# Two decoder layers on one core: both output projections as three float32r products by column halves, with the expert weights loaded at half way and at the last product

## The chip, the cores and the metric

The kernel runs on one core of one Trainium2 chip. The metric is the device time of one execution in microseconds (us), the median of several runs. The core has five engines that run at the same time: TensorE (PE, matrix products into PSUM), VectorE (DVE), ScalarE (ACT), GpSimd (POOL) and SyncE (SP), which here issues nearly all transfers. Sixteen DMA engines move the data between HBM and SBUF.

## What is computed

A causal decoder trunk of two layers over 512 tokens of width 1024, all in float32. Each layer does

```
x = layer_norm(ALPHA * x + mixer(x) @ w_out)
x = layer_norm(ALPHA * x + hierarchical_moe(x))
x = x + sigmoid(x @ w_gate) * (p @ w_proj)
```

In layer 0 the mixer is a retention with four heads beside a causal pooling mixer in four groups; their eight blocks of 128 features form the 1024 features that `ab_w_out` (1024 x 1024) maps. In layer 1 it is a sparse attention with 16 heads over the top 128 keys; `c_w_out` (1024 x 1024) maps its output. The mixture of experts sends each token to two of 32 experts; an expert is a 1024 x 1024 matrix `moe_w_gu` (4.19 MB) and a 512 x 1024 matrix `moe_w_down` (2.10 MB). The kernel loads all 32 experts of a layer.

## The kernel before

The kernel is written engine by engine, in stages; each stage is a block with a barrier at its end, and waits inside it are counts on semaphores. The stages are, for layer 0: the input projection, retention and pooling, the output projection, and routing with the experts; for layer 1: latents and indexer, attention, the output projection, and routing with the experts. P = 128, T = 4 tiles of tokens, KD = 8 blocks of features, NB = 512.

**Split products.** A float32 product on TensorE is two instructions per 512 columns here. The input projection (`split`, line 315 and line 346) and the second output projection use another form: each operand is a high part, which is its copy in the type float32r, and a low part, which is operand minus high part; the product is high x high + high x low + low x high, three float32r instructions. ScalarE makes the high parts (L321, L1964), VectorE (L350) or GpSimd (L1979) the low ones.

**Input projection.** 20 jobs of 128x512 sums on TensorE (L412), five column chunks of four jobs; ScalarE (L334) and VectorE (L376) empty the banks. Jobs 0 to 19 are counted by `pj`.

**Retention and pooling** (L472 to L563). TensorE computes scores (L500), outputs (L507), the pooling maps (L488) and the turned heads (L492). Maps and turned heads pass one after another through PSUM bank 7 in the order of the list `LAST`. TensorE may write job j there only when job j-1 is emptied, and ScalarE empties it with the gain as scale into `MT`, which is `XT` (L557). ScalarE also computes the square root of the variances (L562). VectorE normalises each head (L545) and multiplies with the swish gate (L548). SP loads the two column halves of `ab_w_out`, and then expert 0.

**Output projection** (`out_projection`, L623). For each tile t and column half c, TensorE sums the products of 8 blocks of features (L647) into bank 2t+c. VectorE adds them to ALPHA times x (L670), takes statistics, and normalises a tile when both halves are there (`Norm.dve_tile`, L199: L205, L208, L209). TensorE then turns the tile (L169), ScalarE copies it to `XT` (L176), and TensorE computes the router's logits (L640). The logits of tile t-2 stand behind the first half of tile t, the turn of tile t-1 behind its second. SP loads the router's weights, `load_third_gu` (expert 2 into w3 and w4), and some tables, stores each normalised tile to `x_rows` in HBM (L702), and then issues `then_load`: expert 1, and in layer 1 experts 0 and 1. SP ends the block only when all four stores have landed; it doesn't wait for expert weights.

**Experts.** Routing is a chain on VectorE (L782 to L857). GpSimd then gathers the tokens of an expert from `x_rows` (L883), TensorE turns them (L895) and computes with them (L910, L924). `load_gu` (L436) loads a gate-and-up matrix in two halves of 2.10 MB, `load_dn` (L440) a down matrix of 2.10 MB. There are two buffers for experts: `pair[0]` is wide[1] with slim[0], `pair[1]` is wide[0] with slim[1]; expert 2 uses w3, w4 and `XT`. From expert 3 on, SP issues each piece when TensorE has read the piece that lies in its place. L1163 is the first product behind the last expert.

Of the kernel before, what the change touches and what calls it, by code (L numbers as in the profile page):

```python
# [13 lines left out]
F32 = mybir.dt.float32  # L14
# [8 lines left out]
P = 128  # L23
# [27 lines left out]
def build(nc, A, out):  # L51
    ctx = ExitStack()
    ctx.enter_context(nc.allow_non_contiguous_dma(reason="small vectors to one feature per partition"))
    with ctx:
# [6 lines left out]
        def again(name, of, first, n):  # L61

            return nc.alloc_sbuf_tensor_at(name, [P, n], F32R, offset=home[of] + 4 * first)
# [187 lines left out]
        s_wh, s_wl = sem("w_high"), sem("w_low")  # L251

# [10 lines left out]
        with ExitStack() as first:  # L263
            def early(name, shape, dt=F32):
                return first.enter_context(nc.sbuf_tensor(name, shape, dt))
# [4 lines left out]
            XH, XL = early("x_high", [P, KD, SEQ], F32R), early("x_low", [P, KD, SEQ], F32R)  # L270
            with nc.Block() as block:
                @block.sync
                def _(sp):
# [15 lines left out]
                    sp.dma_start(DEC, A["c_decay"].rearrange("h p n -> p h n")).then_inc(s_dec, 16)  # L289

# [8 lines left out]
                def _(act):  # L299
# [26 lines left out]
                    for j in range(PROJ):  # L326
                        if j % 4 == 0 and 1 <= j // 4 < 4:
                            split(j // 4 + 1)
                        if pj_owner[j] != "act":
# [5 lines left out]
                           .then_inc(pj.sem_of(j), 1)  # L335

                @block.vector
                def _(dve):
# [30 lines left out]
                    for j in range(PROJ):  # L369
# [7 lines left out]
                        if 4 <= j < 12:  # L377
# [4 lines left out]
                            pool_group((j - 4) // 2)  # L382

# [37 lines left out]
        w_out0 = [three(slim[1][:, :], NB), three(wide[0][:, 0:4096], NB)]  # L421
# [37 lines left out]
        MT = XT  # L459
# [10 lines left out]
        mt = Jobs("mixed", ["act"] * len(LAST))  # L470

        with nc.Block() as block:  # L472
            @block.sync
            def _(sp):
                sp.dma_start(PW, A["pool_w"][0].rearrange("g c d -> c g d")).then_inc(s_pool, 16)
                sp.dma_start(w_out0[0], rows(A["ab_w_out"][0, :, 0:NB], NB)).then_inc(s_wout[0], 16)
                sp.dma_start(w_out0[1], rows(A["ab_w_out"][0, :, NB:D], NB)).then_inc(s_wout[1], 16)
                load_gu(sp, 0, 0, 0)
                load_dn(sp, 0, 0, 0)
# [38 lines left out]
            def _(dve):  # L518
                own = Own(dve, "own_ret")
                dve.wait_ge(s_dec, 16)  # L520
                for h in range(RH + 1):
# [8 lines left out]
                    if h >= 1:  # L530
# [17 lines left out]
                        dve.tensor_tensor(RN[:, :, hs], RN[:, :, hs], SG[:, :, hs], ALU.mult).then_inc(s_rn, 1)  # L548

            @block.scalar  # L550
            def _(act):
                act.wait_ge(s_const, 80)
                act.wait_ge(s_gain, 32)
                for j, (kind, i) in enumerate(LAST):
                    mt.wait_full(act, j)
                    k = i if kind == "turn" else 4 + i
                    act.activation(MT[:, k, :], PS[:, 7, :], ACT.Copy, scale=gains[:, k:k + 1])\  # L557
                       .then_inc(mt.sem_of(j), 1)
# [64 lines left out]
        def out_projection(l, products, w_sems, load_first, then_load):  # L623
# [7 lines left out]
            with nc.Block() as block:  # L631
                @block.tensor
                def _(pe):
                    for s in w_sems:
                        pe.wait_ge(s, 16)
# [1442 lines left out]
```

## Time and profile before

| | us |
|---|---|
| median of 3 runs | 1652.06 (1650.83 to 1652.81) |
| profiled execution, its own time | 1653.78 |
| its span | 1651.9 |
| TensorE busy | 1441.9 |
| VectorE busy | 410.2 |
| ScalarE busy | 314.9 |
| GpSimd busy | 207.5 |
| main DMA queue, share of the 16 engines' span | 67.5% |

Times in the rows are counted from the start of the span. A row of the order of time gives start, duration, engine, line of the kernel, operation, what it writes and reads, its tile, the number of instructions, and in brackets the idle time before it with what ended it. Matmuls are pipelined, so durations of successive rows overlap by a little; from start to start is the safer reading. The granted clock is given as a share of TensorE's full 2.4 GHz, so 0.50 is 1.2 GHz.

### The profile page before, as it was taken

The page shows a single profiled execution, that of the slowest core. Times are in us where ns is not written, and L with a number is a line of the kernel's source. Part 1 is how long each engine was busy: PE and PEld are TensorE (multiplying, and loading weights), DVE is VectorE, ACT ScalarE, POOL GpSimd, SP SyncE. Part 2 cuts the span into 40 slices and gives each one's busy share as a digit, 9 for nine tenths or more (in the row PEclk, how much of TensorE's full clock was granted, in tenths as well). Part 3 has the DMA queues.
Part 4 walks back from the last instruction along what each step waited for, and adds up shares of the span by engine and source line. Part 5 has one row for each costly group of instructions (what it writes and reads, how often), then busy time and mean ns, then how long its engine had stood idle before and what let it go on. Part 6 is the DMA issues. An engine that isn't in the chain of part 4 may idle for free. (4 is left out here: it accounts for less than half of the span.)

```text
span 1651.9 us, 17175 instructions
## 1 busy us (share of the span) xinstructions
PE 1441.9 (87%) x6216; PEld 684.8 (41%) x6216; DVE 410.2 (25%) x1020; ACT 314.9 (19%) x642; POOL 207.5 (13%) x327
## 2 busy tenths in 40 slices
PE   6998998998887789879998988989987888889887
PEld 5885463332222233224444456853322323333243
DVE  3424351000000001044068354330000000101172
ACT  3212011111011101012234574111101101101121
POOL 0000001211111111100000253011211111111100
PEclk9999989999999999999999999979999999999989
DMA  7107358999999999994200003299999999999840
GB/s 284 51 26 267 139 193 335 411 426 429 430 429 428 430 429 428 424 371 170 109 1 1 1 2 115 83 426 424 427 431 428 429 429 429 428 429 428 358 171 38
DMA packets 78306, 482.57 MB, mean 292 GB/s; under 512 B 18400, under 2 KB 20452, under 8 KB 45480
## 3 DMA queue, kind: packets, MB, share of 16 engines
q1 hardware_dynamic: 65800, 463.76, 67.5%
q0 software_dynamic: 10240, 16.82, 2.7%
q10 hardware_dynamic: 2208, 1.20, 0.2%
q8 instruction: 38, 0.62, 0.1%
q14 instruction: 20, 0.16, 0.0%
HBM read 474.91 MB, written 23.59 MB: 302 GB/s over the span
## 5 line engine op out<-in xcount | busy, mean ns | idle before, releaser
L910 PE MATMUL PS<-wide,w 128*64 128x512 f32 x1984 | 448.3, 601 | 49.4 <-ACT w L929 29.0
L924 PE MATMUL PS<-slim,w 128*64 128x512 f32 x992 | 252.8, 655 | 78.4 <-issue 77.0
L910 PEld LDWEIGHTS PS<-wide,w 128*64 128x64 f32 x1984 | 136.4, 138 | 329.4 <-issue 255.2
L924 PEld LDWEIGHTS PS<-slim,w 128*64 128x64 f32 x992 | 84.2, 149 | 241.2 <-issue 239.1
L936 DVE TENSOR_TENSOR w<-w,PS 128x256 f32<-128x256 f32 x64 | 27.0, 422 | 543.8 <-ACT w L933 543.8
L933 ACT ACTIVATE w<-PS 128x256 f32<-128x256 f32 x64 | 24.5, 383 | 501.8 <-PE PS L910 501.8
L1174 PE MATMUL PS<-wide,XT 128*128 128x512 f32 x256 | 117.8, 617 | 2.3 <-ACT XT L176 2.3
L1485 ACT ACTIVATE w<-PS,w 128x512 f32<-128x512 f32 x62 | 42.6, 687 | 313.2 <-PE PS L924 313.2
L939 DVE COPY w<-PS 128x256 f32<-128x256 f32 x64 | 27.2, 425 | 297.9 <-PE PS L917 297.9
L1352 POOL COPY w<-w 128x1 uint32 (+1 forms) x62 | 11.2, 181 | 660.3 <-ACT w L1485 660.3
L883 POOL DMA_INDIRECT w<-x_rows,w x64 | 67.2, 1050 | 72.3 <-POOL w L1345 51.6
L1174 PEld LDWEIGHTS PS<-wide,XT 128*128 128x128 f32 x256 | 49.7, 198 | 63.6 <-issue 60.5
L889 POOL DMA_INDIRECT y_rows<-w x62 | 63.6, 1026 | 54.8 <-POOL w L1352 54.8
L176 ACT ACTIVATE XT<-PS 128x512 f32<-128x512 f32 x40 | 21.7, 595 | 143.6 <-PE PS L169 143.6
L895 PE MATMUL PS<-ident,w 128*128 128x128 f32 x256 | 42.4, 289 | 5.6 <-DMA w<-x_rows,w 5.5
L929 ACT ACTIVATE w<-PS 128x512 f32<-128x512 f32 x64 | 38.2, 597 | 41.3 <-PE PS L895 39.6
L412 PE MATMUL PS<-x_high,w_high 128*128 128x512 f32 x96 | 38.2, 398 | 8.5 <-DVE w_low L350 8.5
L917 PEld LDWEIGHTS PS<-ident,w 128*128 128x128 f32 x128 | 20.1, 206 | 57.1 <-issue 53.4
L1975 POOL TENSOR_SCALAR w<-w 128x512 f32<-128x512 f32 (+3 forms) x48 | 26.5, 553 | 112.0 <-DVE w L1928 111.7
L895 PEld LDWEIGHTS PS<-ident,w 128*128 128x128 f32 x256 | 36.6, 210 | 6.9 <-DMA w<-x_rows,w 6.9
L1922 DVE CUSTOM_DVE_ANT_0 w<-PS,w 128x512 f32<-128x512 f32 (+2 forms) x48 | 26.3, 551 | 52.0 <-PE PS L1879 51.9
L1951 ACT ACTIVATE w<-w 128x512 f32<-128x512 f32 (+3 forms) x64 | 35.6, 556 | 16.1 <-DVE w L1922 15.8
(232 smaller groups left out, 1627.8 us busy)
## 6 DMA issues: line engine op xcount, KB each, us to landing
wide<-in_moe_w_gu SPq DMA_DIRECT2D x124, 2048.0 KB, 25.8
slim<-in_moe_w_down SPq DMA_DIRECT2D x62, 2048.0 KB, 25.7
w<-in_moe_w_gu SPq DMA_DIRECT2D x4, 2048.0 KB, 12.2
wide<-in_ple_w_gate SPq DMA_DIRECT2D x4, 2048.0 KB, 14.2
w<-in_ab_w_in SPq DMA_DIRECT2D x2, 2048.0 KB, 14.0
w_in<-in_ab_w_in SPq DMA_DIRECT2D x2, 2048.0 KB, 7.5
x_rows<-X SPq DMA_DIRECT2D x8, 512.0 KB, 2.6
XT<-in_moe_w_down SPq DMA_DIRECT2D x2, 2048.0 KB, 29.1
```

The costliest lines, as they stand in the source:

```text
L412: m = pe.matmul(PS[:, j % 8, :], lhsT, rhs, start=(k == 0 and r == 0), stop=(k == KD - 1 and r == 2))
L883: pool.indirect_dma_start(out=xg[q], out_offset=None, in_=x_half, in_offset=bass.IndirectOffsetOnAxis(ap=index, axis=0), bounds_check=2 * ...
L889: pool.indirect_dma_start(out=y_rows, out_offset=bass.IndirectOffsetOnAxis(ap=index, axis=0), in_=ys[q], in_offset=None, bounds_check=4 * ...
L895: m = pe.transpose(PS[:, q, c * P:(c + 1) * P], xg[q].rearrange("p (f c) -> p c f", c=4)[:, c, :], ident[:, :])
L910: m = pe.matmul(PS[u * SLOTS:(u + 1) * SLOTS, 2 + q, :], xeT[q][:, k, :], gu[k].rearrange("p (a u c) -> p a u c", a=2, u=2)[:, :, u, :], s ...
L924: m = pe.matmul(PS[u * SLOTS:(u + 1) * SLOTS, 6 + q, :], gT[:, k, :], dn[k][:, u * NB:(u + 1) * NB], start=(k == 0), stop=(k == FF // P - 1))
L929: return act.activation(xeT[q].rearrange("p (u c) s -> p c u s", u=2), PS[:, q, :].rearrange("p (c u s) -> p c u s", c=4, u=2), ACT.Copy)
L936: return dve.tensor_tensor(ga, sa, PS[:, 2 + q, FF // 2:FF], ALU.mult)
L939: return dve.tensor_copy(gT.rearrange("p (u c) s -> p c u s", u=2), PS[:, 4 + q, 0:2 * P].rearrange("p (c u s) -> p c u s", c=2, u=2))
L1174: m = pe.matmul(PS[:, self.gate_bank(u), :], XT[:, k, t * P:(t + 1) * P], WG[:, k, c * NB:(c + 1) * NB], start=(k == 0), stop=(k == KD - 1))
L1485: act.activation(ys[q], PS[:, 6 + q, :], ACT.Copy, scale=R["gate_of"][:, bass.ds(expert(q, i), 1)]).then_inc(s_y[q], 1)
L1951: act.activation(g, g, ACT.Exp, bias=nmax[:, i:i + 1], scale=-1.0, accum_out=rsum[:, i:i + 1]).then_inc(s_p, 1)
```

## The change

Both projections run over the column halves first and over the tiles inside them. With half 0 done for all tiles, its weights' places are free, and SP loads expert weights into them (`load_half_way`); the rest is issued when the last product is done (`load_after_products`), ahead of the store of the last tile of rows. The first projection becomes a split one: its weights and `MT` get high and low parts. The weights of half 0 are split at the end of the input projection, those of half 1 and `MT` in the retention stage, where ScalarE writes each bank-7 result twice and GpSimd subtracts; for the last job VectorE makes the low part from PSUM. The parts lie in places that become the buffers of the experts: the low weights of half 0 and the low `MT` in wide[1], the high weights of half 0 in wide[0], those of half 1 in slim[0] (low) and slim[1] (high). So expert 0 can't be loaded in the retention stage any more.

```diff
+            OUT_RAW = [three(again(f"out_raw{c}", of, 0, 4096, F32)[:, :], NB) for c, of in enumerate(("w_high1", "w_low1"))]
+            OUT_LOW = [three(again(f"out_low{c}", of, 0, 4096)[:, :], NB) for c, of in enumerate(("w_high1", "w_low1"))]
+            OUT_HIGH = [three(again(f"out_high{c}", of, 0, 4096)[:, :], NB) for c, of in enumerate(("w_in0", "x_high"))]
+            MT_RAW = three(again("mixed0_raw", "w_low0", 0, 4096, F32)[:, :], SEQ)
+            MT_LOW = three(again("mixed0_low", "w_low0", 0, 4096)[:, :], SEQ)
+            MT_HIGH = three(again("mixed0_high", "x_low", 0, 4096)[:, :], SEQ)
...
+                    pj.wait_full(sp, 15)
+                    for c in range(2):
+                        sp.dma_start(OUT_RAW[c], rows(A["ab_w_out"][0, :, c * NB:(c + 1) * NB], NB))\
+                          .then_inc(s_wout[c], 16)
...
+                        if j in (16, 17):
+                            act.wait_ge(s_wl, len(PIECES))
+                            act.wait_ge(s_wout[0], 16)
+                            for k in range(4 * (j - 16), 4 * (j - 15)):
+                                act.activation(OUT_HIGH[0][:, k, :], OUT_RAW[0][:, k, :], ACT.Copy).then_inc(s_oh, 1)
...
+                    for k in range(KD):
+                        dve.wait_ge(s_oh, k + 1)
+                        dve.tensor_tensor(OUT_LOW[0][:, k, :], OUT_RAW[0][:, k, :], OUT_HIGH[0][:, k, :].bitcast(F32),
+                                          ALU.subtract).then_inc(s_ol, 1)
...
-                sp.dma_start(w_out0[0], rows(A["ab_w_out"][0, :, 0:NB], NB)).then_inc(s_wout[0], 16)
-                sp.dma_start(w_out0[1], rows(A["ab_w_out"][0, :, NB:D], NB)).then_inc(s_wout[1], 16)
-                load_gu(sp, 0, 0, 0)
-                load_dn(sp, 0, 0, 0)
...
+                j = len(LAST) - 1
+                k = row_of(j)
+                dve.wait_ge(s_mh, j + 1)
+                dve.scalar_tensor_tensor(MT_LOW[:, k, :], PS[:, 7, :], gains[:, k:k + 1], MT_HIGH[:, k, :].bitcast(F32),
+                                         ALU.mult, ALU.subtract).then_inc(mt.sem_of(j), 1)
...
+            @block.gpsimd
+            def _(pool):
+                for k in range(KD):
+                    pool.wait_ge(s_oh1, k + 1)
+                    pool.tensor_tensor(OUT_LOW[1][:, k, :], OUT_RAW[1][:, k, :], OUT_HIGH[1][:, k, :].bitcast(F32),
+                                       ALU.subtract).then_inc(s_ol1, 1)
+                for j in range(len(LAST) - 1):
+                    k = row_of(j)
+                    mt.wait_emptied(pool, j)
+                    pool.tensor_tensor(MT_LOW[:, k, :], MT_RAW[:, k, :], MT_HIGH[:, k, :].bitcast(F32), ALU.subtract)\
+                        .then_inc(s_ml, 1)
...
+                act.wait_ge(s_wout[1], 16)
+                for k in range(KD):
+                    act.activation(OUT_HIGH[1][:, k, :], OUT_RAW[1][:, k, :], ACT.Copy).then_inc(s_oh1, 1)
...
-                    act.activation(MT[:, k, :], PS[:, 7, :], ACT.Copy, scale=gains[:, k:k + 1])\
-                       .then_inc(mt.sem_of(j), 1)
+                    k = row_of(j)
+                    act.activation(MT_HIGH[:, k, :], PS[:, 7, :], ACT.Copy, scale=gains[:, k:k + 1]).then_inc(s_mh, 1)
+                    if j < len(LAST) - 1:
+                        act.wait_ge(s_mh, j + 1)
+                        act.activation(MT_RAW[:, k, :], PS[:, 7, :], ACT.Copy, scale=gains[:, k:k + 1])\
+                           .then_inc(mt.sem_of(j), 1)
...
-                    for t in range(T):
-                        for c in range(2):
+                    for c in range(2):
+                        for t in range(T):
                             pairs = products(t, c)
...
-                            if t >= 2 and c == 0:
+                            if c == 1 and t >= 2:
...
                                 logits(t - 2)
-                        if t >= 1:
-                            pe.wait_ge(norm.done, t)
-                            turn.pe(pe, t - 1)
+                            if c == 1 and t >= 1:
+                                pe.wait_ge(norm.done, t)
+                                turn.pe(pe, t - 1)
...
+                    sums.wait_full(sp, T - 1)
+                    load_half_way(sp)
                     for t in range(T):
+                        if t == T - 1:
+                            sums.wait_full(sp, 2 * T - 1)
+                            load_after_products(sp)
                         sp.wait_ge(norm.done, t + 1)
                         sp.dma_start(x_rows[t * P:(t + 1) * P, :], X[:, t, :]).then_inc(s_rows, 16)
                     load_ln(sp, A["ln2_g"][l], A["ln2_b"][l], s_ln)
-                    then_load(sp, sums)
+                    load_dn(sp, l, 1, 1)
...
-                    sp.dma_start(three(wide[0][:, :], D), rows(A["c_w_out"][0], D)).then_inc(s_cwout, 16)
+                    for c in range(2):
+                        sp.dma_start(three(wide[0][:, c * 4096:(c + 1) * 4096], NB),
+                                     rows(A["c_w_out"][0, :, c * NB:(c + 1) * NB], NB)).then_inc(s_cwout, 16)
...
+        def load_first_0(sp):
+            load_third_gu(sp, 0)
+            load_gu(sp, 0, 1, 1, halves=(1,))
+
+        def load_half_way_0(sp):
+            load_gu(sp, 0, 0, 0, halves=(0,))
+            load_gu(sp, 0, 1, 1, halves=(0,))
+
+        def load_after_products_0(sp):
+            load_gu(sp, 0, 0, 0, halves=(1,))
+            load_dn(sp, 0, 0, 0)
+
+        def load_first_1(sp):
+            load_third_gu(sp, 1)
+
+        def load_half_way_1(sp):
+            load_gu(sp, 1, 0, 0, halves=(1,))
+            load_gu(sp, 1, 1, 1, halves=(0,))
+
+        def load_after_products_1(sp):
+            load_gu(sp, 1, 0, 0, halves=(0,))
+            load_dn(sp, 1, 0, 0)
+            load_gu(sp, 1, 1, 1, halves=(1,))
...
         def first_products(t, c):
-            return [(MT[:, k, t * P:(t + 1) * P], w_out0[c][:, k, :]) for k in range(KD)]
+            ts = slice(t * P, (t + 1) * P)
+            return [pair for k in range(KD)
+                    for pair in ((MT_HIGH[:, k, ts], OUT_HIGH[c][:, k, :]), (MT_HIGH[:, k, ts], OUT_LOW[c][:, k, :]),
+                                 (MT_LOW[:, k, ts], OUT_HIGH[c][:, k, :]))]
```

In layer 1 the split weights are laid out by column half in place of by blocks of features (`out_pieces`, `second_products`), with the same number of products.

## Rows read from the trace of the kernel before

**Rows 1.** The page's 40 slices of the span, bytes moved.

```profile
GB/s 284 51 26 267 139 193 335 411 426 429 430 429 428 430 429 428 424 371 170 109 1 1 1 2 115 83 426 424 427 431 428 429 429 429 428 429 428 358 171 38
```

**Rows 2.** TensorE in order of time, first output projection: products, logits, turns.

```profile
159.96 9.97 PE L647 MATMUL PS<-slim,XT 128*128 128x512 f32 x16 [1.18 <-PEq L472]
169.76 7.03 PE L647 MATMUL PS<-wide,XT 128*128 128x512 f32 x16
176.63 7.03 PE L647 MATMUL PS<-slim,XT 128*128 128x512 f32 x16
...
198.11 1.87 PE L640 MATMUL PS<-w,XT 128*128 128x36 f32 x16
199.81 7.11 PE L647 MATMUL PS<-wide,XT 128*128 128x512 f32 x16
...
223.16 1.04 PE L169 MATMUL PS<-ident,X 128*128 128x128 f32 x8
...
227.78 1.97 PE L169 MATMUL PS<-ident,X 128*128 128x128 f32 x8 [0.41 <-DVE X L209]
```

**Rows 3.** TensorE in order of time, second output projection: first product, end of products.

```profile
1013.79 0.47 PE L647 MATMUL PS<-w_out_high,mixed_high 128*128 128x512 f32 x1 [1.69 <-PEq L1869]
...
1062.91 1.04 PE L169 MATMUL PS<-ident,X 128*128 128x128 f32 x8
```

**Rows 4.** TensorE and GpSimd in order of time, layer 0: routing, gather, experts, their end.

```profile
234.85 6.65 PE L724 MATMUL PS<-ident 128*128 128x128 f32 x32 [0.30 <-PEq L631]
...
246.51 1.20 POOL L883 DMA_INDIRECT w<-x_rows,w  x1 [9.49 <-DVE w L857]
...
253.47 0.75 PE L895 MATMUL PS<-ident,w 128*128 128x128 f32 x4 [1.51 <-DMA w<-x_rows,w]
254.90 8.55 PE L910 MATMUL PS<-wide,w 128*64 128x512 f32 x32 [0.69 <-ACT w L929]
...
724.77 2.85 PE L1163 MATMUL PS<-w 64*128 64x512 f32 x12 [0.88 <-ACT w L1514]
```

**Rows 5.** The same in layer 1: one row of TensorE, three of the chain (start, us).

```profile
1074.61 6.62 PE L724 MATMUL PS<-ident 128*128 128x128 f32 x32 [0.30 <-PEq L631]
...
1086.36 8.09 DMA w<-x_rows,w
...
1096.31 9.42 PE PS L910 x32
...
1569.76 1.14 PE PS L1163 x4
```

**Rows 6.** Windows of 5 us: length, busy time of PE, PEld, DVE, ACT, POOL, clock, DMA share, GB/s.

```profile
160.00:165.00 5.00, 5.00 (x6) 2.09 (x7) 0.00 (x0) 0.00 (x0) 0.00 (x0) 0.50 0.41 51
...
255.00:260.00 5.00, 5.00 (x18) 1.61 (x20) 0.00 (x0) 1.15 (x1) 1.05 (x1) 0.71 0.10 31
...
1100.00:1105.00 5.00, 5.00 (x22) 1.51 (x22) 0.00 (x0) 0.00 (x0) 0.00 (x0) 0.90 1.00 418
```

**Rows 7.** Groups by line and shape: durations in ns, least, median, most.

```profile
L557 ACT ACTIVATE XT<-PS,gains x8: 667/687/687, 138.4 to 158.8; 128x512 f32<-128x512 f32 x8
...
L548 DVE TENSOR_TENSOR wide<-wide,w x4: 691/692/694, 142.4 to 157.3; 128x512 f32<-128x512 f32 x4
...
L1979 POOL TENSOR_TENSOR w_out_low<-wide,w_out_high x16: 1266/1274/1282, 933.9 to 1009.2; 128x512 fp32r<-128x512 f32 x16
```

**Rows 8.** Transfers by what they write and read: size, us from issue to landing.

```profile
x_rows<-X SPq DMA_DIRECT2D x8, 512.0 KB, 2.6
...
slim<-in_ab_w_out SPq DMA_DIRECT2D x1, 2048.0 KB, 8.2
wide<-in_ab_w_out SPq DMA_DIRECT2D x1, 2048.0 KB, 12.9
```

**Rows 9.** Gathers (L883), us to landing: until 300 us; then 1000 to 1200.

```profile
DMA to landing us min/median/max: 2.8/6.9/8.1
...
DMA to landing us min/median/max: 5.7/8.3/9.7
```

More of the change, by code:

```diff
@@ L59, in sb, with again @@
             return ctx.enter_context(nc.sbuf_tensor(name, shape, dt))
[L61 to L63 removed]
+        def again(name, of, first, n, dt=F32R):
+            return nc.alloc_sbuf_tensor_at(name, [P, n], dt, offset=home[of] + 4 * first)
         def lasting(name):
@@ L469, in build, with row_of @@
         LAST = [("map", 0), ("map", 1), ("turn", 0), ("map", 2), ("turn", 1), ("map", 3), ("turn", 2), ("turn", 3)]
-        mt = Jobs("mixed", ["act"] * len(LAST))
+        mt = Jobs("mixed", ["act"] * (len(LAST) - 1) + ["dve"])
+        s_oh1, s_ol1 = sem("out_high1"), sem("out_low1")
+        s_mh, s_ml = sem("mixed_high"), sem("mixed_low")
+        def row_of(j):
+            kind, i = LAST[j]
+            return i if kind == "turn" else 4 + i
         with nc.Block() as block:
@@ L621, in build, with out_projection @@
         LG_ALL = PS[:, 0:2 * T:2, 0:NG + NE]
-        def out_projection(l, products, w_sems, load_first, then_load):
+        def out_projection(l, products, w_sems, load_first, load_half_way, load_after_products):
             n = f"out{l}"
@@ L633, in _ @@
                 def _(pe):
-                    for s in w_sems:
-                        pe.wait_ge(s, 16)
+                    for s, loads in w_sems:
+                        pe.wait_ge(s, 16 * loads)
                     def logits(t):
@@ L665, in _ @@
                     dve.wait_ge(s_ln, 64 * l + 32)
-                    for t in range(T):
-                        for c in range(2):
-                            sums.wait_full(dve, 2 * t + c)
+                    for c in range(2):
+                        for t in range(T):
+                            sums.wait_full(dve, c * T + t)
                             xs = X[:, t, c * NB:(c + 1) * NB]
@@ L1611, in _ @@
                 def _(sp):
-                    sp.dma_start(three(wide[0][:, :], D), rows(A["c_w_out"][0], D)).then_inc(s_cwout, 16)
+                    for c in range(2):
+                        sp.dma_start(three(wide[0][:, c * 4096:(c + 1) * 4096], NB),
+                                     rows(A["c_w_out"][0, :, c * NB:(c + 1) * NB], NB)).then_inc(s_cwout, 16)
                     sp.dma_start(DIST, A["c_dist"]).then_inc(s_dist, 16)
@@ L2017, in first_products @@
         def first_products(t, c):
-            return [(MT[:, k, t * P:(t + 1) * P], w_out0[c][:, k, :]) for k in range(KD)]
+            ts = slice(t * P, (t + 1) * P)
+            return [pair for k in range(KD)
+                    for pair in ((MT_HIGH[:, k, ts], OUT_HIGH[c][:, k, :]), (MT_HIGH[:, k, ts], OUT_LOW[c][:, k, :]),
+                                 (MT_LOW[:, k, ts], OUT_HIGH[c][:, k, :]))]
         def second_products(t, c):
-            ts, cs = slice(t * P, (t + 1) * P), slice(c * NB, (c + 1) * NB)
-            high = [WOH[k // 4][:, k % 4, cs] for k in range(KD)]
-            return [pair for k in range(KD) for pair in ((MCH[:, k, ts], high[k]), (MCH[:, k, ts], WOL[:, k, cs]),
-                                                         (MCL[:, k, ts], high[k]))]
-        out_projection(0, first_products, s_wout, before_out(0), after_out(0))
+            ts = slice(t * P, (t + 1) * P)
+            return [pair for k in range(KD)
+                    for pair in ((MCH[:, k, ts], WOH[c][:, k, :]), (MCH[:, k, ts], WOL[:, c * KD + k, :]),
+                                 (MCL[:, k, ts], WOH[c][:, k, :]))]
+        out_projection(0, first_products, [(s, 1) for s in s_wout], load_first_0, load_half_way_0, load_after_products_0)
         layer_end(0, next_layer_loads, lambda sp, s_done: None, True)
```

41 lines of the change are left out of this document (16 added, 25 removed).

## The prediction

> **What bounds the kernel now.** I read the page's 40 slices first, for where the time is spent at all. From slice 7 to 17 and from 26 to 36 the transfers run at about 429 GB/s, slice after slice [rows 1]: these are the two expert stages, and no arithmetic moves them. I then read TensorE's order of time around each projection [rows 2, 3], because the change is there, and the steps from a projection to the first expert product [rows 4, 5]. Last came the 5 us windows at the start of each expert stage [rows 6], which say whether a stream of weights starts at once or waits for a buffer.
>
> The reader is to see two things. An expert needs 6.29 MB (three pieces of 2.10 MB), 14.7 us at 429 GB/s, and TensorE needs less than that, so an expert stage is as long as its stream of weights and starts with the first expert. The stage took 469.9 us in layer 0 (254.90 to 724.77) and 473.5 us in layer 1 (1096.31 to 1569.76) [rows 4, 5]. In layer 0 the transfers fell idle just ahead of the first released buffer (share 0.10 at 255 to 260), in layer 1 they still had a backlog there (1.00 at 1100 to 1105) [rows 6]. So what counts is when the first expert starts, and in layer 1 also the backlog at that time. TensorE's busy share is no guide.
>
> **Layer 0, the stages ahead of the projection.** In the first stage ScalarE and VectorE get eight copies and eight subtractions for the first column half of the weights. The load is issued when group 15 is full; its kind lands 8.2 us after issue, the next 12.9 [rows 8], and four product groups still follow. Sixteen instructions of under 0.7 us on two otherwise free engines fit into them. Cost nothing; without that cover some 5 us.
>
> In the retention stage every ScalarE copy out of bank 7 becomes two, 0.69 us each [rows 7], and TensorE and VectorE wait for it. The eight copies of the second half (5 us) lie ahead of the first bank-7 result and are hidden, GpSimd's subtractions (1.27 us each [rows 7]) too. I followed the timeline with the second copy put in: the first square root is 0.7 late, the second turn 1.4, the last square root 2.2 (it now stands behind both copies of the last map). At the end stand one high copy and one VectorE instruction of about 0.7 where one copy stood. Together **+3.0 us**; bounds 1.5 (only the last two places) and 5.6 (eight times 0.7, nothing hidden). The projection starts at 159.96 + 3.0 = 163.0.
>
> One rule weighs here. The last multiplication on VectorE (0.69 us [rows 7]) has both inputs in SBUF, and GpSimd would now be subtracting beside it; no GpSimd work lies in that stage in the trace of before, so no row shows the pair. The Trainium skill, "SBUF — State Buffer", section "Who interferes with whom", says that a VectorE instruction with two SBUF inputs and a GpSimd instruction that reads SBUF block each other for a whole instruction. By it the sum would rise by up to 1.3 us; by the rows of the engines apart, by nothing. I take nothing.
>
> **Layer 0, the projection.** Before it ran 63.2 us, from 159.96 to 223.16 [rows 2]. The same loop in layer 1, already split in three float32r products, with the same turns and logits in between, ran 49.1 us, 1013.79 to 1062.91 [rows 3]. Layer 0 began at the lower level of 1.2 GHz (granted 0.50 at 160 to 165 [rows 6]) and its first 16 matmuls took 9.8 us to the next row, where the next 16 took 6.9 (169.76 to 176.63) [rows 2]. I keep 2.9 us for that, since little goes ahead of it after the change either: 52.0 us. The new order puts the logits of tile 1 behind the last product, where they stood before it: 1.70 us (198.11 to 199.81 [rows 2]). The last product then ends at 163.0 + 52.0 - 1.7 = 213.3, not 223.2. VectorE's norm of a tile is done 4.6 us after its product (223.16 to 227.78 [rows 2]), and a product group of a split half lasts about 49.1 / 8 less turns, 5.4 us: the norm fits between and stalls nothing. The logits moved back fill TensorE's wait for the last norm.
>
> **What the stores now wait for.** SP issues two loads of 2.10 MB at the last product in layer 0 and three in layer 1, and then the store of the last tile of rows, in the same queue. The block can't end before that store lands. Two loads of this size issued 0.5 us apart landed 4.7 apart, as 8.2 and 12.9 us [rows 8]: the queue works in order. Two loads take 12.8 us from the first issue (13.4 less 0.6 for the 0.26 MB issued ahead of them), a third 4.8, the store of 0.52 MB 1.2 behind them (2.6 alone [rows 8]). With overlaps of issue and landing I put the next block's start 14.0 us behind the last product in layer 0 and 18.8 in layer 1. Before it was 11.7 us in both (223.16 to 234.85 and 1062.91 to 1074.61 [rows 2 to 5]), with TensorE last.
>
> Layer 0: next block at 227.3, which is 7.6 us earlier. From there to the gather of the first expert's tokens nothing changes (234.85 to 246.51 [rows 4]): 238.9. Before, that gather ran beside the weight loads and took 6.9 us; gathers landed in 2.8 us at the least and mostly in some 8 in full traffic [rows 9]. Now the loads are nearly through: 14.0 us hold the last store, then 3.1 MB of norm vectors and weights and 2.1 MB, 12.2 us, to about 239. I take 4.0 us, bounds 2.8 and 6.9. It lands at 243.0, not 253.5: **-10.5 us**. The stream of 29 experts then starts from a free queue, as before, so the stage keeps its 469.9 us.
>
> Layer 1: the projection has the same matmuls. Its last product ends 1.7 earlier, at 1061.2, the next block starts at 1080.0 in place of 1074.6 (+5.4), the gather goes out at 1091.8 and takes 4.0 in place of 8.1 [rows 5]: it lands **+1.3 us** later. But before, 15.7 MB (norm vectors, six pieces of two experts, the third down matrix) were issued behind the last norm, from 1068 on, and lasted past the first release. Now 12.1 MB are issued from 1061.2 on, 28.2 us at 429 GB/s, through at about 1091, and the first expert frees its buffer into an idle queue as in layer 0. The stage was 3.6 us longer than that of layer 0; of this 0.9 is in the first 32 matmuls (9.42 against 8.55 [rows 4, 5], clock), which I don't count: **-2.8 us**. Bounds for layer 1 together: +4 (gather 8.1 as before, nothing else lost) to -5 (block end not late).
>
> Edits at no cost: the two halves of the attention's output weights, loaded by two transfers in a stage where the queue moves 109 GB/s and less [rows 1]; the order of their split, same instructions; loads at half way, some 25 us into the projection, behind 6.3 MB (14.7 us) that are through by then; the clearing of six more semaphores.
>
> **Sum.** -10.5 + 1.3 - 2.8 = -12.0 us. The profiled execution took 1653.78 us with a span of 1651.9; the median of the runs is 1652.06, 1.7 below it. Differences inside the span carry over: 1652.06 - 12.0 = **1640.0**.
>
> **Rivals.**
> 1. The last store is not late: the stores land early enough and TensorE stays last. For it: the load of expert weights and the store move in different directions. Against: the landings in order [rows 8]. Layer 0 would gain 2 us more and layer 1 5 more: 1633.
> 2. Gathers stay slow (6.9 and 8.1 us) although the loads are through, because the third down matrix (2.1 MB) is issued at the same block start. For it: every gather in traffic took some 8 us [rows 9]. Against: by my account it is through when the gather goes out. 1640 + 2.9 + 4.1 = 1647. The Trainium skill, "DMA: Bandwidth & Descriptors", section "Queues, rings and completion order", says that a DMA engine serves its queues in turn, packet by packet, but that a semaphore's increment lands only behind every earlier write of that engine. By that rule the last load of a queue would hold the gather's signal back, which is this rival; 6.9 and 8.1 us in traffic agree with it but don't single it out.
> 3. The other side: TensorE stays at 1.2 GHz through the first projection. It goes into it from a stage that leaves it idle longer than before, and three fast products per step fill it no better than two slow ones. At that level the 8 groups cost 8 x 5.4 = 43 us more, of which 2.9 are in the sum: 1680. It decides from 12 us of loss, a little over two groups more at the lower level. Against it: layer 1's same products were at full clock throughout, and layer 0's rose within 6 us [rows 3, 6].
> 4. The change buys nothing: the retention stage grows by its upper bound, the block ends late and gathers stay slow, all short of slower: some 1650.
>
> **Chances.** The sum 0.58, rival 1 0.14, rival 2 0.20, rival 3 0.04, rival 4 0.04. The forecast is 1640. Alone it would be 1635 to 1645; to take in rivals 1 and 2 the range is 1632 to 1648. The measurement tells no change from one of 0.2% (3.3 us). Faster: the first three and most of the fourth, 0.93; same 0.03; slower 0.04.
>
> **What would show it.** The projection of layer 0 starting near 163.0 and its last product ending near 213; 5.4 us a group; SP, not TensorE, last at the end of both projection blocks, by 2 to 8 us; the last store landing some 9 us (layer 0) and 14 us (layer 1) after its issue, in place of 2.6; the first gathers in 3 to 5 us; an idle gap in the transfers ahead of the first release in both layers; both expert stages near 470 us. The prediction is wrong if a half stalls on the norm, if the new splits are not done when their stage ends, if the clock stays low, or if an expert stage grows longer than 474 us, since then something other than the stream's start sets its length.

## The result and the profile after

The changed kernel ran in 1643.79 us (median of 5; 1642.13 to 1645.24) beside 1652.81 us for the kernel before on the same chip (5 runs). The ratio is 0.9946 [0.9932, 0.9961], so it is faster by 9.0 us; I had forecast 12.0 less, 1640.0. The profiled span fell from 1651.9 to 1641.9 us.

TensorE and GpSimd in order of time, changed kernel (answers to [rows 2 to 5]):

```profile
164.76 0.77 PE L695 MATMUL PS<-out_high,mixed_high 128*128 128x512 f32 x1 [2.17 <-PEq L498]
...
213.46 1.87 PE L688 MATMUL PS<-w,XT 128*128 128x36 f32 x16
...
219.28 1.95 PE L169 MATMUL PS<-ident,X 128*128 128x128 f32 x8
222.40 3.63 PE L688 MATMUL PS<-w,XT 128*128 128x36 f32 x16 [1.17 <-ACT XT L176]
228.70 2.69 PE L778 MATMUL PS<-ident 128*128 128x128 f32 x11 [2.67 <-PEq L679]
...
240.60 1.22 POOL L937 DMA_INDIRECT w<-x_rows,w  x1 [9.35 <-DVE w L911]
...
239.68 3.62 PE L1470 MATMUL PS<-w,ranks 128*128 128x32 f32 x16 [0.47 <-DVE w L911]
243.12 4.51 PE L778 MATMUL PS<-ident 128*128 128x128 f32 x24
247.46 0.64 PE L949 MATMUL PS<-ident,w 128*128 128x128 f32 x4
248.79 7.09 PE L964 MATMUL PS<-wide,w 128*64 128x512 f32 x32 [0.69 <-ACT w L983]
...
717.52 2.85 PE L1217 MATMUL PS<-w 64*128 64x512 f32 x12 [0.88 <-ACT w L1568]
...
1006.26 0.47 PE L695 MATMUL PS<-w_out_high,mixed_high 128*128 128x512 f32 x1 [1.69 <-PEq L1925]
...
1053.41 1.87 PE L688 MATMUL PS<-w,XT 128*128 128x36 f32 x16
...
1073.54 6.56 PE L778 MATMUL PS<-ident 128*128 128x128 f32 x32 [7.32 <-PEq L679]
...
1085.04 1.14 POOL L937 DMA_INDIRECT w<-x_rows,w  x1 [9.33 <-DVE w L911]
...
1084.18 1.97 PE L1470 MATMUL PS<-w,ranks 128*128 128x32 f32 x16 [0.47 <-DVE w L911]
1085.99 4.55 PE L778 MATMUL PS<-ident 128*128 128x128 f32 x24
1090.38 0.64 PE L949 MATMUL PS<-ident,w 128*128 128x128 f32 x4
1091.71 3.65 PE L964 MATMUL PS<-wide,w 128*64 128x512 f32 x16 [0.69 <-ACT w L983]
...
1561.16 2.85 PE L1217 MATMUL PS<-w 64*128 64x512 f32 x12 [0.88 <-ACT w L1568]
```

L778 is the filler, products of the identity that nobody reads (L724 before); L1470 are the gate sums just ahead of its last stretch. The landmarks as a ledger (us from the span's start; "before" from [rows 2 to 5]; "forecast" is the prediction's own clock, which started the first stage where before did; the turn was put at the gather's landing). The last column is how much earlier or later the step came out, measured from the landmark above it:

| landmark | before | forecast | after | step, after minus before |
|---|---|---|---|---|
| first score product | 130.65 | 130.65 | 131.68 | +1.0 |
| layer 0: first projection product | 159.96 | 163.0 | 164.76 | +3.8 |
| behind the last product | 223.16 | 213.3 | 213.46 | -14.5 |
| next block (filler) | 234.85 | 227.3 | 228.70 | +3.6 |
| gather issued | 246.51 | 238.9 | 240.60 | +0.2 |
| first turn of the gathered | 253.47 | 243.0 | 247.46 | -0.1 |
| mix (end of experts) | 724.77 | 714.3 | 717.52 | -1.2 |
| layer 1: first projection product | 1013.79 | | 1006.26 | -0.3 |
| behind the last product | 1062.91 | | 1053.41 | -2.0 |
| next block | 1074.61 | | 1073.54 | +8.4 |
| gather issued | 1086.36 | | 1085.04 | -0.3 |
| first turn of the gathered | 1094.49 | | 1090.38 | -2.8 |
| mix | 1569.76 | | 1561.16 | -4.5 |
| end of the span | 1651.9 | | 1641.9 | -1.4 |

The reader is to see that the large terms came as forecast: the first projection is 14.5 us shorter, both blocks end later after their last product, and TensorE waited there for the block's end (2.67 and 7.32 us ahead of L778, put down to PEq, where before it was 0.30). The row that breaks the forecast is the one of "-0.1": the gather was issued 5.9 us earlier and the turn came 6.0 earlier, although the gather itself had become 4 us faster.

Landings in the changed kernel, us from issue: the last store of rows in layer 0 and in layer 1, the two loads issued at L0's last product, then gathers until 250 us and in 1060 to 1092 (answers to [rows 8, 9]).

```profile
DMA to landing us min/median/max: 9.2/9.2/9.2
...
DMA to landing us min/median/max: 14.1/14.1/14.1
...
DMA to landing us min/median/max: 7.8/7.8/7.8
...
DMA to landing us min/median/max: 12.9/12.9/12.9
...
DMA to landing us min/median/max: 2.7/2.8/3.2
...
DMA to landing us min/median/max: 2.8/2.9/3.0
```

In layer 0 the second load was issued at 214.02 and landed at 226.9; the store behind it in the queue was issued at 219.08 and landed at 228.3, 1.4 us after the load. Windows of the changed kernel around the first releases (answers to [rows 6]):

```profile
245.00:250.00 5.00, 4.31 (x27) 3.40 (x28) 1.95 (x8) 1.84 (x2) 0.66 (x2) 0.85 0.10 38
...
1090.00:1095.00 5.00, 4.31 (x25) 2.03 (x26) 0.00 (x1) 1.88 (x2) 1.26 (x2) 1.00 0.11 30
1095.00:1100.00 5.00, 4.06 (x20) 1.27 (x17) 0.42 (x1) 0.38 (x1) 0.00 (x0) 1.00 0.71 232
```

The DMA share is 0.11 at 1090 to 1095 in layer 1: the backlog is gone, as forecast, and the expert stage from its first product took 469.5 us (before 473.5), like layer 0's 468.7 (before 469.9).

### The profile page after: what moved, and what is told of

The parts are those of the page before. It is cut to its first block and busy times, and to the rows that moved or that the text cites. A ratio compares the mean times of both kernels' runs of the same rounds, so it can differ in the third digit from the quotient of the medians.

```text
span 1641.9 us, 17364 instructions
## 1 busy us (share of the span) xinstructions
PE 1426.5 (87%) x6280; PEld 699.3 (43%) x6280; DVE 417.6 (25%) x1029; ACT 328.7 (20%) x665; POOL 227.1 (14%) x342
## 5 line engine op out<-in xcount | busy, mean ns | idle before, releaser
L964 PE MATMUL PS<-wide,w 128*64 128x512 f32 x1984 | 444.0, 596 | 48.8 <-ACT w L983 29.1
L971 PEld LDWEIGHTS PS<-ident,w 128*128 128x128 f32 x128 | 20.1, 206 | 56.5 <-issue 52.9
L434 PE MATMUL PS<-x_high,w_low 128*128 128x512 f32 x96 | 38.3, 399 | 0.0
## 6 DMA issues: line engine op xcount, KB each, us to landing
out_raw<-in_ab_w_out SPq DMA_DIRECT2D x2, 2048.0 KB, 10.5
```

The costliest lines, as they stand in the source:

```text
L434: m = pe.matmul(PS[:, j % 8, :], lhsT, rhs, start=(k == 0 and r == 0), stop=(k == KD - 1 and r == 2))
L964: m = pe.matmul(PS[u * SLOTS:(u + 1) * SLOTS, 2 + q, :], xeT[q][:, k, :], gu[k].rearrange("p (a u c) -> p a u c", a=2, u=2)[:, :, u, :], s ...
```

## The experiments

Each is an edit of the changed kernel; ratios are to the kernel before on the same chip (medians 1652.6 to 1653.9). Where only one execution was timed, the text says so. The steps of e1 and e2 come from their longest execution (1650.07 and 1640.96 us, 4.1 and 2.0 above their medians), those of e8 from its shortest.

**The filler taken out (e1).** Theory: TensorE's filler between the routing and the gathered tokens is late.

```diff
-                    keep_running(pe, 12, 5)
```

> The changed kernel without the 12 filler products (24 instructions) that TensorE does between the gate sums and the first expert, in both layers. Theory A: in the changed kernel the first gather lands 2.8 to 3.2 us after its issue, while the first turn of tokens starts 6.9 us (layer 0) and 5.4 us (layer 1) after it, when the filler is done. So the turn comes some 3.5 and 2.3 us earlier, the stream of weights starts as much earlier, and the kernel gains 4 to 6 us against 1643.8. Rival B: the filler keeps the clock up; without it the first 32 expert products take 9 to 14 us in place of 7.1 and give the gain back, total within 2 us of the changed kernel. Rival C: the gather lands later than its record says and the turn keeps its time, with idle TensorE ahead of it.

Measured: 1646.0 us (1644.23 to 1650.07), 0.9954 [0.9940, 0.9968]: nothing gained over the change's 0.9946.

```profile
245.00 1.13 PE L949 MATMUL PS<-ident,w 128*128 128x128 f32 x4 [2.00 <-DMA w<-x_rows,w]
246.82 9.99 PE L964 MATMUL PS<-wide,w 128*64 128x512 f32 x32 [0.69 <-ACT w L983]
...
721.53 2.85 PE L1217 MATMUL PS<-w 64*128 64x512 f32 x12 [0.88 <-ACT w L1567]
```

```profile
245.00:250.00 5.00, 4.31 (x12) 1.73 (x14) 1.70 (x8) 1.88 (x2) 1.51 (x3) 0.50 0.18 63
```

The turn now waits for the gather (2.00 <-DMA) and comes 3.2 us after its issue (241.76), not 6.9, so the filler was what held it. But the granted clock at 245 to 250 was 0.50 (0.85 with filler), the first 32 expert products took 9.99 us in place of 7.09, and from their start to the mix it was 474.7 us against 468.7. Most of this lies at the start: the first two steps from one expert's turn to the next took 13.1 and 13.8 us, against 9.7 and 12.1. From the block's start to the mix layer 0 took 491.7 us against 488.8, layer 1 488.4 against 487.6. The filler delays the turn, and in layer 0 the clock pays for it; in layer 1 the difference of 0.8 us is too small to say.

**The last store of rows ahead of the loads (e2), or on ScalarE's queue (e3).**

```diff
-                        if t == T - 1:
-                            sums.wait_full(sp, 2 * T - 1)
-                            load_after_products(sp)
                         sp.wait_ge(norm.done, t + 1)
                         sp.dma_start(x_rows[t * P:(t + 1) * P, :], X[:, t, :]).then_inc(s_rows, 16)
+                    load_after_products(sp)
```

> The changed kernel with the store of the last tile of rows issued ahead of the loads that follow the last product (these then wait for the last norm too, 5 us later). Theory A: the store behind the loads ends both projection blocks; it should land in some 2.6 us in place of 9.2 and 14.1, the next block starts some 3 us (layer 0) and 8 us (layer 1) earlier, with TensorE last. The loads have 5 us less, so the gathers run beside them and take 6 to 8 us in place of 3, which eats most of the filler's cover only: gain 5 to 10 us against 1643.8. Rival D: in layer 1 the stream still has its backlog at the first release, so the expert stage is 3 us longer again and the gain is 2 to 5 us.

> The changed kernel with the loads at the last product as they are, but the store of the last tile issued from ScalarE's DMA queue. Theory A (order inside one queue is what holds the store): it lands in 3 to 5 us and the next block starts 2.5 and 7.5 us earlier, gain 5 to 9 us against 1643.8. Rival E (the DMA engines are simply full, whatever the queue): it lands in 8 us or more and little is gained.

Measured: e2 1639.0 us (1636.97 to 1640.96), 0.9906 [0.9891, 0.9921]; e3 1640.4 (1638.48 to 1641.59), 0.9915 [0.9902, 0.9929]. Both intervals end below the change's, which begins at 0.9932. In e2 no store took more than 4.0 us to land, and TensorE is last at the block's end (0.30 <-PEq):

```profile
1063.77 3.62 PE L688 MATMUL PS<-w,XT 128*128 128x36 f32 x16 [1.17 <-ACT XT L176]
1067.69 5.30 PE L776 MATMUL PS<-ident 128*128 128x128 f32 x32 [0.30 <-PEq L679]
```

The block ended 12.8 us behind the last product in layer 1 (20.1 in the change), and 14.4 in layer 0 (15.2). Its last logits run at 1.2 GHz (granted 0.50 at 1063.5 to 1067.6), 3.62 us in place of 1.87. In e3 the store had a queue of its own and still took 8.4 and 9.4 us (alone 2.6 [rows 8]):

```profile
DMA to landing us min/median/max: 8.4/8.4/8.4
...
DMA to landing us min/median/max: 9.4/9.4/9.4
```

In layer 0 it landed at 228.1, 0.2 ahead of the last load (issued 214.62, 13.7 us); in layer 1 at 1066.9, 4.1 ahead of it. So standing in the same queue cost 4.7 of the 14.1 us in layer 1, but only 0.8 of the 9.2 in layer 0. In both layers the store landed within 1 us of the second load (228.3 and 1066.1), with a third load in flight or without. The sixteen engines were full meanwhile (share 1.00 at 225 to 228), but that this alone holds the store is not shown. The Trainium skill, "DMA: Bandwidth & Descriptors", section "Queues, rings and completion order", says that an engine serves its queues in turn; the store overtaking the third load in layer 1 agrees, and by itself it doesn't explain the 8.4 us of layer 0.

**No subtraction by GpSimd in the retention stage (e4).** It leaves out the low parts of seven blocks of `mixed` (they are set to zero), so GpSimd reads nothing there.

> The changed kernel, but GpSimd writes zeros into the low parts of seven of the eight blocks of the mixed features in place of subtracting (the low parts are left out, so the first projection has only two of its three products in effect); GpSimd then only writes SBUF. Theory A: the two multiplications of VectorE by the swish gate that took 1.54 and 1.64 us because GpSimd was reading go back to 0.69 us, and the retention stage, 33.1 us from its first product to the projection's, loses 0.5 to 1.7 us. Rival: they were slow for another reason and stay at 1.5 us.

One execution: 1641.85 us. Of the order of time, VectorE and GpSimd in the changed kernel:

```profile
149.51 1.54 DVE L570 TENSOR_TENSOR wide<-wide,w 128x512 f32<-128x512 f32 x1
...
149.23 1.27 POOL L587 TENSOR_TENSOR mixed_low<-mixed_raw,mixed_high 128x512 fp32r<-128x512 f32 x1 [1.86 <-ACT mixed_raw L605]
...
160.67 0.69 DVE L570 TENSOR_TENSOR wide<-wide,w 128x512 f32<-128x512 f32 x1
```

Two of VectorE's gate multiplications (1.54 here, 1.64 at 155.83) began beside a subtraction of GpSimd and took over twice their 0.69 us; in e4 all took 0.69. Here the rule weighed in the prediction (the Trainium skill, "SBUF — State Buffer", "Who interferes with whom") agrees with the trace: they exclude each other. But in e4 the stage is 32.9 us against 33.1: the delays lie beside a longer wait and cost 0.2 us, less than the 0.5 to 1.7 expected.

**Layer 1's projection as before (e6), and both layers' expert loads issued late (e7).** e6 gives layer 1 its tile-first order and old loads back. e7 keeps the new order and the split product, and issues all loads behind the last store, without the wait at half way:

```diff
-                    sums.wait_full(sp, T - 1)
-                    load_half_way(sp)
...
-                            load_after_products(sp)
...
+                    load_half_way(sp)
+                    load_after_products(sp)
                     load_dn(sp, l, 1, 1)
```

> The changed kernel with the second projection as it was: tiles outside, column halves inside, logits where they stood, and its expert weights issued after the last norm (their order among themselves is that of the changed kernel). Layer 0 is as changed. Theory A: in layer 1 the block end, 8.4 us later after the last product, eats what the earlier product end (2.0), the faster gather and the shorter expert stage (4.0) give. So this kernel takes the same as the changed one within 2 us (ratio to before 0.993 to 0.996), its second block ends 11.7 us after the last product, the gather takes 8 us and the expert stage 473 us. Rival: the change in layer 1 has a worth of its own; then this kernel is 3 us or more slower than the changed one.

> The changed kernel with all loads of half way and of the last product issued behind the last norm's rows, in both layers; the split products and the order by column halves stay. Theory A: both blocks end 12.9 us after the last product (TensorE last). But layer 0 now has 15.7 MB behind its last norm, as layer 1 had before: its gather takes 7 to 8 us, its expert stage 472 to 474 us in place of 469. Layer 0: block end -2.3, gather and its filler +1, stage +4; layer 1: -7, +2.5, +4. Together within 3 us of the changed kernel, 1642 to 1647. Rival: the early loads are what makes the change faster; then this one falls back to 1648 or more.

Measured: e6 1645.7 us (1645.08 to 1647.16), 0.9956 [0.9942, 0.9969]; e7 1646.2 (1645.12 to 1646.37), 0.9955 [0.9941, 0.9968]. Neither can be told from the change by its interval. From the first projection product to the mix, layer 0 took 564.8 us before, 552.8 in the change, 553.7 in e6 and 554.2 in e7: without the early loads layer 0 keeps all but 1.5 us of its gain. Layer 1's steps say why:

| layer 1, us | before | change | e6 | e7 | e2 |
|---|---|---|---|---|---|
| projection | 49.1 | 47.2 | 49.1 | 48.8 | 47.2 |
| last product to next block | 11.7 | 20.1 | 11.7 | 12.6 | 12.8 |
| next block to mix | 495.2 | 487.6 | 494.8 | 495.0 | 490.4 |
| sum | 556.0 | 554.9 | 555.5 | 556.3 | 550.4 |

The early loads shorten gather and stage by 7.5 us, and the store behind them makes the block 8.4 longer; with the 2.0 of the shorter projection layer 1 gains 1. That is no more than the swing of this projection: in e1, e4 and e7, with the same products, it took 48.8 us in place of 47.2, its start being at the lower level (granted 0.66 at 1007 to 1012 in e7, 1.00 in the change at 1006 to 1011). So the 48.8 of e7 is no effect of its edit. In e7 the stream is still full at 1095 to 1100, where the change's share was 0.71 (above); the gathers took 6.9 us and the stage from the first product 475.3:

```profile
1095.00:1100.00 5.00, 3.37 (x20) 1.62 (x20) 0.84 (x2) 0.98 (x2) 0.00 (x0) 1.00 1.00 424
```

**The raw copy of each `mixed` block first, the high part from SBUF behind it (e8).** A bank is then free after one ScalarE copy again, and the square root, too, stands behind one copy only.

```diff
-                    act.activation(MT_HIGH[:, k, :], PS[:, 7, :], ACT.Copy, scale=gains[:, k:k + 1]).then_inc(s_mh, 1)
                     if j < len(LAST) - 1:
-                        act.wait_ge(s_mh, j + 1)
                         act.activation(MT_RAW[:, k, :], PS[:, 7, :], ACT.Copy, scale=gains[:, k:k + 1])\
                            .then_inc(mt.sem_of(j), 1)
...
+                    if j < len(LAST) - 1:
+                        mt.wait_emptied(act, j)
+                        act.activation(MT_HIGH[:, k, :], MT_RAW[:, k, :], ACT.Copy).then_inc(s_mh, 1)
```

> The changed kernel, but in the retention stage ScalarE first makes the float32 copy out of bank 7, which frees the bank, then the square root, and only then the high part, from that copy in SBUF. Theory A: the retention stage grew by 3.8 us because the second copy stands in the way of the bank and of the square root; now it should be 1.0 to 2.0 us longer than before (30.3 to 31.3 us from its first product to the projection's), so the kernel gains 2 to 3 us against the changed one, about 1641. Rival: the stage is longer because of GpSimd's and VectorE's shared use of SBUF or the later end of the last job alone; then it stays at 32 to 33 us.

Measured: 1641.65 us (1640.42 to 1645.67), 0.9935 [0.9921, 0.9948]. TensorE at the turned heads, e8:

```profile
150.37 0.66 PE L514 MATMUL PS<-ident,wide 128*128 128x128 f32 x4 [0.78 <-ACT mixed_raw L603]
...
160.46 0.77 PE L699 MATMUL PS<-out_high,mixed_high 128*128 128x512 f32 x1 [2.17 <-PEq L498]
```

and in the change:

```profile
153.48 0.66 PE L514 MATMUL PS<-ident,wide 128*128 128x128 f32 x4 [1.50 <-ACT mixed_raw L605]
```

The wait for bank 7 is 0.78 us as before, not 1.50, and the stage 30.45 us (before 29.3, change 33.1). So 2.6 of its 3.8 us were the second copy ahead of the bank's release and of the square root; how they share them was not tested. In the timed ratio this is not resolved against the change.

**Filler ahead of the last logits (e9), and all remedies together (e10).** e9 is e2 with ten 128-column products of the identity ahead of each of the last two groups of logits. e10 is e9 with e8's order of copies.

```diff
+                    keep_running(pe, 5, 1)
                     logits(T - 2)
                     pe.wait_ge(norm.done, T)
                     turn.pe(pe, T - 1)
+                    keep_running(pe, 5, 1)
                     logits(T - 1)
```

> The kernel with the store ahead of the loads, and in addition five filler products on TensorE ahead of the last two groups of logits, where it waits 1.17 us for ScalarE's copies. Theory A: the tail after the last product takes 12.8 to 14.4 us because its last turn and logits run at 1.2 GHz (1.95 and 3.63 us in place of 1.07 and 1.87); with the filler they run at 2.4 GHz and the next block starts 10 to 11 us after the last product, so this one gains 4 to 6 us against the store alone. Rival: so small a filler doesn't hold the clock; the tail stays at 13 us or gets longer by the filler, 0 to 2 us.

> All three remedies in one kernel: the last store of the rows issued ahead of the loads, ten filler products ahead of the last logits groups in both blocks, and the raw copy of the retained rows evicted first. Theory (the costs lie one behind the other and add): the filler with the early store gave 1633.9 us and a retention stage of 33 us; the raw copy first shortened that stage from 33.08 to 30.45 us, so 1633.9 - 2.6 = 1631.3 us, ratio to before 0.987, block ends 10.3 us behind the last products in both layers, retention stage 30.4 us. Rival (the raw copy's 2.1 us between the timed medians, 1643.8 to 1641.7, was a swing of the first stage's clock): 1633.5 to 1634 us although the stage is shorter.

Measured: e9 1633.9 us (1632.82 to 1634.51), 0.9881 [0.9866, 0.9896]; e10 1631.9 us (1631.65 to 1634.06), 0.9876 [0.9859, 0.9894]. The order of time of e10:

```profile
211.94 1.87 PE L692 MATMUL PS<-w,XT 128*128 128x36 f32 x16
213.64 1.07 PE L169 MATMUL PS<-ident,X 128*128 128x128 f32 x8
214.55 1.28 PE L782 MATMUL PS<-ident 128*128 128x128 f32 x10
215.88 1.98 PE L692 MATMUL PS<-w,XT 128*128 128x36 f32 x16
217.69 1.07 PE L169 MATMUL PS<-ident,X 128*128 128x128 f32 x8
218.60 1.28 PE L782 MATMUL PS<-ident 128*128 128x128 f32 x10
219.94 1.98 PE L692 MATMUL PS<-w,XT 128*128 128x36 f32 x16
222.21 3.81 PE L782 MATMUL PS<-ident 128*128 128x128 f32 x32 [0.30 <-PEq L683]
...
241.06 0.75 PE L953 MATMUL PS<-ident,w 128*128 128x128 f32 x4 [1.29 <-DMA w<-x_rows,w]
```

The filler fills the wait of 1.17 us for the copy, the last turn takes 1.07 us and the last logits 1.98, where the change had 1.95 and 3.63; the granted clock was 1.00 at 219.5 to 223.8 in e9, where e2 had 0.50 at 221 to 228. The blocks end 10.3 us behind the last product in both layers, less than the 11.7 of before. Part is given back: the gathers go out sooner and meet the loads again, 6.7 us (layer 0) and 7.1 (layer 1) to landing of the first, and with the store first layer 0 takes 491.1 us from block to mix (change 488.8). The retention stage of e10 is 30.5 us (131.88 to 162.36), of e9 33.1; e10's median is 2.0 below e9's, its ratio only 0.0005, and the intervals lie over each other. That the stage is shorter is shown, that the whole kernel is by as much is not.

## Why the prediction was right in the main and 3.8 us off

**Retention stage, forecast +3.0, came +3.8.** Inside the bounds (1.5 to 5.6). The mechanism was the one named, the second copy out of bank 7 (e8: 2.6 of it). The SBUF rule, which I took as nothing, was worth 0.2 (e4).

**First stage, forecast 0, came +1.0.** In the runs of the changed kernels the first score product began between 130.0 and 131.9 us with the same code ahead of it; the profiled change is at the upper end. I count it as a swing.

**Projection, forecast 163.0 to 213.3, came 164.76 to 213.46.** 48.7 us, not 50.3: its start at 1.2 GHz cost 1.5 us over layer 1's 47.2, not the 2.9 kept for it. That is luck of this execution: the granted clock at 164 to 169 was 0.61, in e2 0.50, and over all changed kernels the same products took 48.6 to 50.1 us, in six of ten 49.6 or more. This term carries the result: -14.5 us, while e6, e7 and the ledger show layer 1 and the early loads to be worth 1 to 2. The new order alone gave layer 1's projection 2.0 us, so by this estimate some 12 of the 14.5 are the split. It was not timed alone.

**Block ends, forecast 14.0 and 18.8, came 15.2 and 20.1.** The cause was right: the store landed 9.2 and 14.1 us after issue, where "some 9" and "14" were named, and TensorE waited 2.7 and 7.3 us. From the first load's issue to the store's landing it took 14.6 and 19.5 us; the forecast took 14.0 and 18.8 for this and the steps beside it, which are 0.2 us ahead of it and 0.4 behind. e2 moved the store and gained: -7.3 us at layer 1's block end. In layer 0 there is little behind it (0.8 us), for TensorE's own tail was next; I had put TensorE's tail at no more than the 11.7 us of before, and with one more group of logits behind the last product and the low clock it is 12.6 to 14.4 (e2, e7).

**The step that failed: "I take 4.0 us ... It lands at 243.0, not 253.5: -10.5 us."** The landing was right: issued at 240.60, landed 2.8 later at 243.4 (and in layer 1, +0.9 us against +1.3 forecast, counted from the first projection product). What was wrong is that the landing starts the expert. Between routing and the gathered tokens TensorE runs 24 filler instructions. The kernel before has them too, in TensorE's order of time:

```profile
247.40 4.55 PE L724 MATMUL PS<-ident 128*128 128x128 f32 x24
```

There they ended at 251.95 and the turn waited 1.51 us more for the gather [rows 4], so they were hidden; with a gather of 2.8 us the filler is last, 4.1 us behind the landing in layer 0 (243.4 to 247.46) and 2.5 in layer 1 (1087.9 to 1090.38). The difference of the two is the clock: ahead of the filler the gate sums took 3.62 us in layer 0 and 1.97 in layer 1, and in e3 and e4, where they took 1.97 in layer 0 too, the turn came 5.3 and 5.2 us after the gather's issue, not 6.9. So 2.5 of the 4.1 us are the filler, the rest is a swing. Nor would the gap be free: in e1 the turn came as forecast and the first products ran slow, and the time was no better than the change's. I had priced the gather and not asked what is late next.

**Expert stages, forecast 469.9 and -2.8 in layer 1, came 468.7 and 469.5** (-1.2 and -4.0 from the first expert product). The idle queue at the first release is there, and e6 and e7, with a backlog, kept 475.0 and 475.3 in layer 1: the explanation holds.

**The sum.** Up to the first turn of layer 0 the profile shows -6.0 in place of -10.5. Of the 4.5 lost, the filler is 4.1 (the slow gate sums in it), the block's end 1.2, the first stage 1.0, retention 0.8 and the step to the gather 0.3; the projection gave 1.6 back and the faster gather 1.2 (rounding leaves 0.1). In layer 1 up to the turn it is +3.4 in place of +1.3: filler 2.5 and block end 1.3, less 1.2 by the gather and 0.5 by projection and routing. From turn to mix the stages came 1.2 and 1.7 better than forecast, and code that is unchanged 0.3 (between the layers) and 1.4 (behind the last mix; over all runs of changed kernels that tail swung from 80.6 to 82.2 us). 4.5 + 2.1 - 1.2 - 1.7 - 0.3 - 1.4 = 2.0: the span fell by 10.0, not 12.0. That it came so near is in part luck: 6.6 us were lost up to the two turns, and 4.6 won by terms that I had at nothing or smaller, 1.7 of them in code that the change doesn't touch. The other 1.8 us of the 3.8 lie outside the profile: the medians differ by 9.0, 1.0 less than the spans, and the runs of before had a median 0.75 above the one that the forecast started from.

**Slips in the working, none above 0.5 us in a layer.** The two loads of [rows 8] were issued at 131.02 and 131.57, so their landings lie 5.2 us apart, not 4.7. The 0.6 us taken off for the 0.26 MB issued ahead of them was too much: the change's pair took 13.3 us, not 12.8. 3.6 less 0.9 is 2.7, not 2.8. Rival 1 reckons layer 0 with a tail of 11.7 us and layer 1 with 1.7 more. The slices 7 and 17 of [rows 1] moved 411 and 371 GB/s, being the stage's edges.

**The rivals.** Rival 1 (last store not late) is excluded by the landings. Rival 2 (gathers stay slow) is not what happened here, though its time, 1647, lay nearer than its mechanism: in layer 0 the turn was as late as if it had. Its condition is seen in e2, e7, e9 and e10, where gathers met a queue still full and took some 7 us. Rival 3 (TensorE at 1.2 GHz) and rival 4 are excluded by the ledger. What stays open is why e3's store, alone in its queue, took 8.4 us with two loads in flight and hardly more with three.

## What to carry to other kernels

When a transfer on the path gets faster, list everything that its waiter still has to do, filler included; what was hidden by 1.5 us becomes the bound when the transfer is 4 us faster. A load moved ahead of a small store in the same queue makes the store as late as the load: put first what a barrier waits for. And in a tail of short products with waits between, look at the granted clock before counting instructions: two stretches of 1.28 us of filler in the waits were cheaper than the last groups at half clock (e9 beside e2).

## What the runs showed of the hardware that was not expected

- A tail of 36-column products with waits of 1.17 us went at half clock (granted 0.50): 3.63 us for 16 products in place of 1.87. Ten products of 128 columns (1.28 us) in each wait kept the full clock (granted 1.00 in e9) in both layers (e9, e10), and the block ended 4.2 (layer 0) and 2.6 us (layer 1) sooner than in e2.
- A 0.52 MB store in a queue of its own took 8.4 us beside 4.2 MB of loads, where in an idle queue it takes 2.6. Beside 6.3 MB it took 9.4, where in the loads' queue it took 14.1. Why a queue of its own gave so little beside two loads stays open.
- Gathers of an expert's rows take 2.7 to 3.2 us when the loads are through. In the changed kernels where they met the loads their medians were 6.1 to 7.3 us (before 7.0 and 8.9), and 4.9 us in e3's layer 1, where they met the end of them.
